# Recurrent scan of a Trainium2 kernel: compact operands instead of zero-padded pairs, and how they are turned

## The reference

```python
def step(s, inp):
    r_t, w_t, k_t, v_t, kk_t, b_t = inp
    sa = jnp.einsum('bhij,bhj->bhi', s, kk_t)
    s = s * w_t[:, :, None, :] - sa[..., None] * b_t[:, :, None, :] + v_t[..., None] * k_t[:, :, None, :]
    y = jnp.einsum('bhij,bhj->bhi', s, r_t) if emit else None
    return s, y
```

## Time and profile before

| | |
|---|---|
| runs | 4702.28, 4691.91, 4700.87 us, median 4700.87 |
| the profiled execution's own time | 4704.09 us |
| its span | 4702.3 us, mean granted clock of PE 0.939 |
| busy, share of the span | PE 87%, PEld 72%, DVE 46%, ACT 32%, POOL 17% |
| scan stage | from about 1877 us (its first DMA issue) to 2710 us (first instruction of the next stage) |
| scan input | 160 loads of FE, 192 KB each, by SP |

### The profile page before, as it was taken

One profiled execution on the slowest core, in us unless ns is written; L12 is line 12 of the kernel. 1 busy time (PEld: TensorE's weight loads), 2 busy tenths in 40 slices (PEclk: granted clock), 3 DMA queues, 4 the chain that ended last, 5 costly groups with the idle time before them and its releaser, 6 DMA issues. The chain is left out here.

```text
span 4702.3 us, 74174 instructions
## 1 busy us (share of the span) xinstructions
PE 4112.0 (87%) x29857; PEld 3383.3 (72%) x29857; DVE 2156.8 (46%) x3952; ACT 1523.6 (32%) x3236; POOL 815.8 (17%) x725
## 2 busy tenths in 40 slices
PE   8999797998989985898887879997895988999998
PEld 2789787997889872787776724446794766888786
DVE  3233375344522228677777764475313553111234
ACT  2111254655521117333333350005212553221133
POOL 0000353100100661434444460001000000000000
PEclk9999898999999997999999979998897989999999
DMA  8233432102332566212222050214224132111122
GB/s 321 74 102 115 111 80 60 32 18 92 126 99 92 191 221 250 62 35 49 49 49 49 22 188 25 76 49 170 91 92 165 49 119 72 49 45 49 38 89 69
DMA packets 291264, 439.23 MB, mean 93 GB/s; under 512 B 76980, under 2 KB 210708, under 8 KB 286399
## 3 DMA queue, kind: packets, MB, share of 16 engines
q1 hardware_dynamic: 290664, 429.81, 28.9%
q10 hardware_dynamic: 288, 5.07, 0.3%
HBM read 315.76 MB, written 124.03 MB: 94 GB/s over the span
## 5 line engine op out<-in xcount | busy, mean ns | idle before, releaser
L387 PE MATMUL g_acc<-g_wh,l_x_high 128*128 128x320 f32 (+5 forms) x1824 | 593.5, 325 | 40.2 <-DVE g_wl L53 33.7
L387 PE MATMUL g_acc<-g_wl,l_x_high 128*128 128x320 f32 (+5 forms) x1824 | 591.4, 324 | 0.0
L387 PE MATMUL g_acc<-g_wh,l_x_low 128*128 128x320 f32 (+5 forms) x1824 | 591.0, 324 | 0.0
L387 PEld LDWEIGHTS g_acc<-g_wh,l_x_high 128*128 128x128 f32 x1824 | 347.3, 190 | 48.6 <-DVE g_wl L53 34.3
L387 PEld LDWEIGHTS g_acc<-g_wl,l_x_high 128*128 128x128 f32 x1824 | 348.1, 191 | 2.8
L387 PEld LDWEIGHTS g_acc<-g_wh,l_x_low 128*128 128x128 f32 x1824 | 347.4, 190 | 2.4
L435 DVE COPY g_o<-g_acc 128x320 f32<-128x320 f32 (+6 forms) x120 | 62.7, 524 | 576.9 <-PE g_acc L387 539.4
L411 ACT COPY g_o<-g_acc 128x320 f32<-128x320 f32 (+6 forms) x120 | 54.6, 455 | 772.7 <-PE g_acc L387 730.7
L3088 PE MATMUL ffi_acc<-l4a_x_high,ffi_wh 128*128 128x512 f32 x704 | 274.9, 390 | 11.9 <-DVE ffi_wl L53 11.9
L3088 PE MATMUL ffi_acc<-l4a_x_high,ffi_wl 128*128 128x512 f32 x704 | 274.6, 390 | 0.0
L3088 PE MATMUL ffi_acc<-l4a_x_low,ffi_wh 128*128 128x512 f32 x704 | 274.6, 390 | 0.0
(11 more groups left out here) (508 smaller groups left out, 9572.8 us busy)
## 6 DMA issues: line engine op xcount, KB each, us to landing
scan_F<-s_FE SPq DMA_DIRECT2D x160, 192.0 KB, 3.7
s_FE<-feat_f SPq DMA_DIRECT2D x10, 2304.0 KB, 7.8
ffi_w<-in_w_ffn_in SPq DMA_DIRECT2D x44, 512.0 KB, 3.8
g_cu<-s_U SPq DMA_DIRECT2D x24, 768.0 KB, 5.1
pj_o<-s_O SPq DMA_DIRECT2D x26, 512.0 KB, 4.6
front_w<-in_attn_ada_w SPq DMA_DIRECT2D x8, 1536.0 KB, 12.1
front_w<-in_rec_ada_w SPq DMA_DIRECT2D x8, 1536.0 KB, 12.5
g_wr<-in_w_ffn_out SPq DMA_DIRECT2D x44, 256.0 KB, 2.6
```

Source lines behind the costliest of these rows:

```text
L387: mm = pe.matmul(acc[r][:, 0:it["n"]], left, right, start=(k == 0 and q == 0), stop=(k == kt - 1 and q == 2))
```

## The change

All main operands become compact, [128, 4, 64]: one head in each partition half, no zero blocks. `pairs` takes `left[hb, :]`. Writes of two halves become one instruction. LW, As, MR, the memsets of zero blocks, `warm`, the identity products of the last chunk, `Linked` waits and `ready` go. `scaled` is now called per direction: d = 0 after step 4, d = 1 after step 7 (before: all after step 7). `exps` and `sums` move likewise, and POOL's order is new. M and R are separate tensors with separate products, A (power) in bank 1 and B (term for R) in bank 2. In step 5 PE computes the far power twice, once with its operands swapped, which is its turned form; ACT copies both to far_two at once, and `quarters` goes.

```diff
 def pairs(to, c0, n, left, right, start=True, stop=True):
     for hb in HALF:
-        mm = pe.matmul(to[hb, c0:c0 + n], left[hb, hb], right[hb, :], start=start, stop=stop)
+        mm = pe.matmul(to[hb, c0:c0 + n], left[hb, :], right[hb, :], start=start, stop=stop)
...
-    pe.matmul(b[0][:, 0:256], tri[:, 2 * d, :], lw, start=True, stop=True)
+    for hb in HALF:
+        pe.matmul(b[0][hb, 0:256], tri[hb, 2 * d, hb], flat(f[hb, 3, :, :]), start=True, stop=True)
     for h in range(NP2):
-        mm = pe.matmul(b[2][:, h:h + 1], LW[d][:, h, :], one[:, :], start=True, stop=True)
+        mm = pairs(b[0], 256 + h, 1, f[:, 3, h, :], one[:, :])
...
+def turn(n, d):
+    for to, left, need in ((1, qk[d][n % 2], 2), (2, qa[d], 4)):
+        pe.wait_ge(s["scaled"], 4 * n + need)
...
+        for x in range(2):
+            for h in range(NP2):
+                for hb in HALF:
+                    mm = pe.matmul(b[to][hb, x * 256 + h * C:x * 256 + (h + 1) * C], left[hb, x, h, :], ident[hb, hb], start=True, stop=True)
+        mm.then_inc(s["turned"], 1)
...
 def step(n, k):
     for d in range(2):
...
+        if k in A_AT:
+            for h in range(NP2):
+                if k == 5:
+                    pairs(a, h * C, C, SS[d][:, h, :], far[d][:, h, :])
+                    mm = pairs(a, 256 + h * C, C, far[d][:, h, :], SS[d][:, h, :])
+                elif k == 6:
+                    mm = pairs(a, h * C, C, far_two[d][:, 0, h, :], far_two[d][:, 1, h, :])
+                else:
+                    mm = pairs(a, h * C, C, SS[d][:, h, :], (mid if k == 1 else M)[d][:, h, :])
+            mm.then_inc(s["step_a"], 1)
+        if k in B_AT:
...
+            for h in range(NP2):
+                left = {6: far_two[d][:, 1, h, :], 7: SX[d][:, h, :]}.get(k, SS[d][:, h, :])
+                mm = pairs(b, h * C, C, left, R[d][:, h, :])
+            mm.then_inc(s["step_b"], 1)
...
-pieces = {1: ((0, 0), (0, 1)), 2: ((0, 2),), 4: ((0, 3),), 5: ((1, 0), (1, 1)), 6: ((1, 2), (1, 3))}
+pieces = {1: ((0, 0), (0, 1)), 2: ((0, 2),), 4: ((0, 3), (1, 0)), 5: ((1, 1),), 6: ((1, 2), (1, 3))}
...
     mix_w(n - 1)
-    for x in range(3):
-        turn(n, x)
+    turn(n, 0)
     mix_u(n - 1)
-    turn(n, 3)
-    grams(n)
+    turn(n, 1)
+    grams(n, 0)
     mix_s(n - 1)
+    grams(n, 1)
...
-    if k in (2, 3):
+    if n + 1 < NCH and k in (2, 4):
+        sums(n + 1, k // 2 - 1)
...
             @block.scalar
-                        if n + 1 < NCH and k in (2, 3):
-                            exps(n + 1, k - 2)
+                        if n + 1 < NCH and k in (3, 6):
+                            exps(n + 1, k // 3 - 1)
...
             @block.vector
+def after(n, k):
+    for d in range(2):
+        if k in (2, 3, 4, 6):
+            added(n, k, d)
+        if k in (1, 2, 3):
+            dve.wait_ge(s["power"], 5 * n + A_AT[k])
+            turned(d, M[d])
+        if k == 4:
+            dve.wait_ge(s["r_out"], 4 * n + 3)
+            turned(d, R[d])
...
-        if n + 1 < NCH:
-            for x in range(4):
-                scaled(n + 1, x)
+            if n + 1 < NCH and k in (4, 7):
+                scaled(n + 1, 0 if k == 4 else 1)
```

More of the change, by code:

```diff
@@ L1382, in sums @@
                     mm.then_inc(s["sums"], 1)
[L1384 to L1394, removed]
-                        src = qa[d][:, x // 2, :, :] if x % 2 == 0 else qk[d][n % 2][:, 1 - x // 2, :, :]
-                        for h in range(NP2):
-                            mm = pe.transpose(b[to][:, h * P:(h + 1) * P], src[:, h, :], ident[:, :])
-                        mm.then_inc(s["turned"], 1)
@@ new lines, in grams @@
+                def grams(n, d):
+                    s, b = e[d], bank[d]
+                    pe.wait_ge(s["a_out"], n + 1)
+                    pe.wait_ge(s["kb_out"], n + 1)
+                    pe.wait_ge(s["exps"], 4 * n + 4)
+                    for x, to in ((1, 2), (0, 0)):
+                        for h in range(NP2):
+                            mm = pairs(b[to], h * P, P, KB[d][:, x, h, :], AR[d][n % 2][:, h, :, :].rearrange("p x t -> p (x t)"))
+                        mm.then_inc(s["grams"], 1)
@@ L1417, in step @@
                         if k == 5:
+                            pe.wait_ge(s["ss_out"], 5 * n + 5)
                             pe.wait_ge(s["parts"], 4 * n + 4)
-                        for h in range(NP2):
-                            if k in (2, 3, 6):
-                                mm = pairs(bank[d][1], h * P, P, SS[d][:, h, :], MR[d][:, h, :, :].rearrange("p x t -> p (x t)"))
-                            else:
-                                of = {1: mid[d][:, h, :], 5: far[d][:, h, :]}.get(k, MR[d][:, h, 1, :])
-                                mm = pairs(bank[d][1], h * C, C, (SX if k == STEPS else SS)[d][:, h, :], of)
@@ L1585, in _, with shift @@
             def _(pool):
-                def blocks(n):
+                def shift(n, d):
+                    s = e[d]
+                    pool.wait_ge(s["exps"], 4 * n + 2)
+                    pool.tensor_tensor(ex[d][:, 0, :, :], ex[d][:, 0, :, :], ex[d][:, 1, :, :], ALU.mult).then_inc(s["shifted"], 1)
+                pool.wait_ge(const_in, 32)
+                pool.wait_ge(cleared, 5)
+                for d in range(2):
+                    shift(0, d)
+                for n in range(NCH):
@@ L1616, in kept @@
+                    if n + 1 < NCH:
+                        shift(n + 1, 0)
                     for d in range(2):
[L1617 to L1621 removed]
@@ L1693, in u_out, with turned @@
                         dve.tensor_scalar(flat(Un[d][:, :, :]), b[3][:, 256:512], -1.0, None, ALU.mult).then_inc(s["u_out"], 1)
[L1695 to L1714 removed]
+                def turned(d, of):
+                    dve.transpose(SS[d][:, :, :], of[:, :, :]).then_inc(e[d]["ss_out"], 1)
                 def start(n):
```

339 lines of the change are left out of this document (124 added, 215 removed).

## The result

The changed kernel takes 4522.39 us (median of 4 runs, 4520.69 to 4523.67), the kernel before in the same series 4701.57 us (4691.91 to 4702.49): a ratio of 0.9623, 95% interval 0.9606 to 0.964. Forecast were 4523 us and a range of 4455 to 4600. The profiled execution took 4520.69 us, its span is 4518.9 us.

What follows compares the result with a forecast made beforehand. The scan was taken as bound by the chain PE, ACT, DVE, PE with DVE's work in it. From the profiled 4704 us, 200 came off across the chunks and 19 was added for the clock: 4523 us, 8-in-10 range 4455 to 4600.

Steps and rivals of the forecast that it cites:

- What bounds it: Scan: the chain PE, ACT, DVE, PE and DVE's work in it; DVE falls from 30.6 to about 15.8 us a chunk.
- The removed instructions stood in the chain one for one: DVE in the scan: argument that removed instructions count in full, such as 20 to 10 turns at 0.44, -4.4 us.
- rival 1: Steps of the scan: rounds stay long, 2.9 us, or corner turns cost 6.8; 3.2 us a chunk more, 4587 us; 18%.
- Corner turns at 3.7 us a chunk: PE's turns: 64 calls at 0.058 us, 3.7 us against 4.3 for transposes; 6.8 if the two halves do not overlap.
- The new wait: Ahead of step 1: PE idles 2.4 us because POOL's mid of d0 queues behind the wait for GA of d1.
- Step 2 at 16.7: Chunk schedule: DVE's state ends at 16.1, M of d0 is turned at 16.6, step 2 runs 16.7 to 18.6 us.
- The clock: PE after the thin stretch 12.0 to 16.7: a drop on steps 2 and 3, charged 1 us x 19 = 19.
- Warming products: Chunks 0 to 4: products go; chunks 1 to 4 take 29.3 instead of 42.9 us, three places in chunk 0 save 4.6 and more.
- 3 (4962): PE in the scan: clock drops to 1.2 GHz and stays, issue doubles to 53 us a chunk, 4962 us; 4%.
- 4 (4577): Head of the chunk: scaling per direction brings nothing, head stays at 17.1 us, only the steps gain, 4577 us; 8%.
- 2 (4434): Scan PE-bound: POOL's wait and the clock cost nothing, a chunk is PE's issue plus 1 us, 27.5, 4434 us; 10%.
- Giving up the transpose mode: PE's turns: by the skill's 4x rule 32 transposes cost 0.9 us, turns lose 2.8 us a chunk, 4579 us; trace disagrees.

Runs made afterwards that it cites:

- Run 7: Changed kernel with step 5's far power turned by DVE again in 32x128 pieces, PE's 16 second products taken away; 4577.25 us.
- run 8: Changed kernel with each 128x256 DVE turn issued as two of 64 rows, ten more instructions a chunk; 4557.09 us.
- run 2: Changed kernel with each corner turn on PE issued twice, 64 more calls a chunk; 4598.37 us.
- Run 3: Changed kernel with POOL's mid made right behind R of its direction, ahead of the wait for GA of d1; 4519.32 us.
- Run 5: Changed kernel with the grams of both directions ahead of mix_s, as in the kernel before; 4466.93 us.
- run 4: Changed kernel with 36 identity products filling PE's idle gap between the grams of d1 and step 1; 4507.98 us.
- run 10: Changed kernel with POOL's mid made early and DVE's state update moved between the turns of R of d0 and d1; 4485.64 us.
- Run 1: Kernel before without its warming products and the last chunk's identity products; 4690.79 us, ratio 0.9976.
- run 6: Changed kernel with the scaling of both directions behind step 7, as before the change; 4515.4 us.
- run 11: Changed kernel with both grams ahead of mix_s and POOL's mid made early too; 4476.86 us.

## Why the prediction was right, and where it was not

**The size.** 4523 forecast, 4522 measured. The stage's gain was 178.3 us against a net 181. The table above shows that no part is off by more than 3 us, so large errors do not cancel between the parts of the stage. Inside a chunk some of about 1 us do, as told below.

**Steps of the schedule,** forecast and measured, from the start of mix_w:

| | forecast | measured |
|---|---|---|
| grams of d1 begin | 10.3 | 10.65 |
| mid of d0 begins on POOL | 13.5 | 13.9 |
| step 1 | 14.4 | 14.8 |
| M of d0 turned (start) | 16.1 | 16.4 |
| step 2 | 16.7 | 17.8 |
| step 3 | 19.9 | 21.0 |
| step 5 | 25.2 | 26.0 |
| end of step 7 | 31.0, with the clock 32.0 | 31.8 |

- *What bounds it* was right: the work DVE had put into the chain. PE's waits for DVE went from 64.4 us in 400 to 3.0. Run 7 prices the quarters of k = 5 at 55 us; scaling, KB and TT at full height have no run of their own. "The removed instructions stood in the chain one for one", my argument against rival 1, is not shown: in run 8, with DVE this empty, only 40% of ten more turns comes out at the end. What the same turns cost in the kernel before, where DVE was at 30.6 us of 40, no run tests.
- *Corner turns at 3.7 us a chunk*: right, 29 ns a row, and run 2 measured 76 us for 64 more calls in each chunk. The upper bound, 6.8, is out.
- *The new wait*: right in place and size (2.18 us, forecast 2.4), wrong in what holds it. **The step that failed** is "mid of d0 has been possible since 8.4 but is queued behind the wait for GA of d1. This is the new wait of the change": it reads as one holder, and as a wait that any such change would have. Run 3 took that queueing away for 3 us. My own schedule had M of d0 turned only at 16.1, after the state, which does not move with mid, so I should have seen that the path to step 2 runs GA of d1, R of d1, its turn, the state. The total did not suffer, because step 2 was placed by DVE anyway. Nor did the prediction ask what had made GA of d1 late: the grams of d1 behind mix_s, where the kernel before did not have them. Run 5 puts them back for 55 us less.
- *Step 2 at 16.7* came at 17.8, although M was turned by 16.9. What fills the time is the low clock: step 1 and the two pieces of mix_y behind it take 3.01 us (2309.28 to 2312.29, the pieces' rows 0.46 us long instead of 0.28), where 32 rows at 29 ns and two pieces of 0.35 would be 1.6. In the next chunk, at full clock, step 2 follows step 1 after 2.10 us (2340.63 to 2342.73), so the low clock costs 0.9 us here. The clock's charge falls one place ahead of where I put it, on step 1 and the pieces.
- *The clock*: 1 us a chunk charged, 0.7 measured (run 4), because the drop comes in some chunks only. The size was the right one: the chunk shown above has a drop and 0.2 us of stalls and takes 31.8 us, and of the two rows below the first is a chunk with a drop and stalls of 1.47 us, 33.49, the second one with neither, 30.33. A drop thus costs some 1.3 (31.8 - 0.2 - 30.3) to 1.7 us (33.5 - 1.5 - 30.3) in these, and 1.2 us on average over seven chunks of each kind (31.8 - 30.6, the table at run 10). Chunks 1 to 19 have 11 drops, which makes 13 us, as run 4 has it. Windows from Wm copy to Wm copy of the changed kernel:

```profile
2164.01:2197.50 33.49, 29.58 (x849) 28.52 (x845) 15.09 (x37) 10.56 (x29) 11.29 (x14) 0.95 0.27 66
2327.45:2357.78 30.33, 27.86 (x847) 26.89 (x844) 15.07 (x37) 10.55 (x29) 11.29 (x14) 1.00 0.26 63
```

- *Not in my sum*: stalls of PE between two products of one run with nothing to wait for, 10.8 us in 400 (7.6 + 3.2 above), some 0.9 us a chunk of 31.9. They lie on the path: the changed kernel's chunks 5 to 18 are from 30.3 to 33.5 us long, and with their stalls taken off they fall into two narrow groups, 30.3 to 31.0 at full clock and 31.6 to 32.0 with a drop. **They were paid for by chance:** the clean chunk takes 30.3 us where the schedule had 31.0, and 30.3 + 0.7 for the clock + 0.9 is the measured 31.9, as 31.0 + 1.0 was the forecast 32.0.
- *Warming products*: the gain in chunks 1 to 4 came (51.3 us, 50 forecast). Run 1 adds what I had not weighed: in the old schedule they had held the clock at 1.00 instead of 0.83, so their price was 1.9 us a chunk net. The new schedule has 0.96 in these chunks without them.
- *Rivals.* 1 (4587) fell: run 2 has the corner turns at 3.7 us, and from step 1 to the end of step 7 the timeline has 17.0 us (14.8 to 31.8), 2.4 a step, where the rival wanted 2.9. 3 (4962) fell: the clock is 0.96 to 0.97 in the scan. 4 (4577) fell for a reason of its own: scaling per direction indeed brings nothing (run 6), but the head does not hang on it; turn d0 starts without a wait either way. 2 (4434) was not this kernel; run 5 comes near it, 33 above.
- *Giving up the transpose mode* cost nothing: 64 corner calls took 3.7 us and 32 transposes, 0.134 us apart, had taken 4.3. The prediction set the transpose against the wrong product, one with 64x64 weights. Its like is the 128x128 product of the identity in the warming groups, here 12 calls at full clock in the kernel before:

```profile
1926.12 2.94 PE L1475 MATMUL scan_bank<-main_ident 128*128 128x128 f32 x24
```

  With the last row's 0.275 us taken off that is 0.116 us a row and 0.232 a call, 1.7 times a transpose. The change loses nothing by it because a corner turn leaves out the blocks that nobody reads: two 64x64 calls, 0.116 us, do the work of one transpose. The Trainium skill ("TensorE: Matmul & The Clock Gate", Terms) calls the transpose mode 4x faster for FP32; the direction agrees with these rows, the size does not. By that figure of the Trainium skill, an estimate, a transpose would cost 0.058 us and the sum would be 4560, not 4579; measured are 4522.

## What to carry to other kernels

When a wait has a named releaser, ask what else is late by the same event. Here POOL's mask and DVE's state both stood behind one late copy; removing either order gave 3 and 11 us, both 37, and making the event itself earlier 55. An idle gap on PE costs its length only if what follows could come earlier (run 3: 2.4 us at step 1, next to nothing at the end), and the clock behind it besides (run 4: 14 us); fillers pay only where the gap stays. Compare runs chunk by chunk at the same clock before calling two effects more than their sum. And test each part of a change that does several things at once: this one gained 179 us and held a new order of the grams that cost 55. What that order would have cost with DVE as loaded as before, no run tests.

## What had not been expected of the hardware

- PE stalls in the middle of a run of equal products, up to 1.4 us, put down to "issue". The kernel before shows none in its scan; the changed kernel has 19, 14.0 us together, and its versions have them too (8.6 us in 400 in run 5, 11.0 in run 11). One stands in chunk 0, in the timeline of PE:

```profile
1898.00 1.31 PE L1349 MATMUL scan_bank<-scan_AR,scan_KB 64*64 64x128 f32 x20 [1.34 <-issue]
```

  The page counts 252 packets on the first instruction queue (q8), 218 before. The trace's DMA records say more: in the scan a packet of 16 KB comes every 4.9 us there, and every 8.4 us in the kernel before. All 19 stalls end from 2.2 to 2.9 us behind the start of such a packet, where by chance one in seven would; of the 190 stalls in the other versions of the changed kernel 186 end from 2.2 to 3.0 us behind one. So the engine most likely waits there for its instructions; no run changed their number or place to test it.

- DVE's two state multiplications take 1.35 us, and 1.48 in run 5, while POOL's masks run beside them, and 0.74 in run 10, where POOL waits during it. The two sums ahead of them, which read one operand from PSUM, take 0.72 to 0.75 in all three, with POOL's masks beside them. Likewise POOL's two far masks, beside the multiplications, take 1.78 us and its two mids 1.41, for the same size; in run 10, with no multiplication beside them, the two far masks take 1.41 too. (The Trainium skill, "GPSIMD Engine Reference", Specifications, has POOL share its SBUF interfaces with DVE and contend with DVE instructions that have two SBUF inputs; the rows agree, the multiplications being of that kind and the sums not.) No run tested it by itself.
- Height is free on DVE and POOL as taken: GK of 128x512 takes 1.264 us, of 64x512 1.265.
